# SBUF layout of a two-block transformer kernel: small tensors first, tiles at chosen offsets modulo 1024 bytes

## The reference

```python
x = first_block(x, ...)     # 1 layer: x += rms_norm(concat(attention(h), mlstm(h) gated) @ w_out)
                            #          x += rms_norm(square(relu(rms_norm(x) @ w_up)) @ w_down), d_ff 4096
x = second_block(x, c, ...) # 2 layers: mod = silu(c) @ ada_w + ada_b; differential attention (4 heads),
                            #   31-tap depthwise convolution, both gated and projected; then
f_gate, f_up = jnp.split(h2 @ w_ffn_in[l], 2, axis=-1)          # d_ff 2816
x = x + (1.0 + gate2) * ((jax.nn.silu(f_gate) * f_up) @ w_ffn_out[l])
```

## Time and profile before

| | |
|---|---|
| median of 3 runs | 1080.71 us (1077.39, 1080.71, 1085.57) |
| profiled execution, its time and span | 1080.6 us |
| granted TensorE clock, mean | 0.994 |
| PE busy / PE weight loads busy | 1058.0 us / 1007.3 us |
| DVE / ACT / POOL busy | 833.6 us / 525.7 us / 29.8 us |
| HBM read | 227.29 MB, 211 GB/s over the span |

### The profile page before, as it was taken

One profiled execution on the slowest core, in us unless ns is written; L12 is line 12 of the kernel. 1 busy time (PEld: TensorE's weight loads), 2 busy tenths in 40 slices (PEclk: granted clock), 3 DMA queues, 4 the chain that ended last, 5 costly groups with the idle time before them and its releaser, 6 DMA issues.

```text
span 1080.6 us, 19232 instructions
## 1 busy us (share of the span) xinstructions
PE 1058.0 (98%) x8174; PEld 1007.3 (93%) x8174; DVE 833.6 (77%) x1117; ACT 525.7 (49%) x625; POOL 29.8 (3%) x54
## 2 busy tenths in 40 slices
PE   7999999999999999999999999999999999999998
PEld 6878899999998989989999999999898899999998
DVE  5878699988775899968898887869999576555552
ACT  5554665554424544554644433464456455444441
POOL 5100000000000010000000000000000000000000
PEclk9999999999999999999999999999999999999998
DMA  8566348889893464428599998846442375666551
GB/s 278 166 215 235 117 176 298 281 288 307 292 353 116 161 200 130 145 88 303 182 368 311 331 335 295 271 135 230 161 156 79 118 254 184 197 190 193 173 175 39
DMA packets 137473, 230.37 MB, mean 213 GB/s; under 512 B 7107, under 2 KB 60715, under 8 KB 137389
## 3 DMA queue, kind: packets, MB, share of 16 engines
q1 hardware_dynamic: 135060, 227.05, 62.1%
q0 software_dynamic: 1408, 0.79, 0.4%
q10 hardware_dynamic: 921, 1.32, 0.4%
HBM read 227.29 MB, written 1.06 MB: 211 GB/s over the span
## 4 chain that ended last, share of the span: by engine, by line
PE 71%; DVE 18%; ACT 7%; DMA 2%; issue 1%; SPq 1%; DVEq 0%; POOL 0%; ACTq 0%
PE mm L435 66%; DVE lo L1296 7%; DVE cacc L1386 5%; ACT hi L840 3%; PE mm L478 1%; DMA raw<-in_w_in_dram 1%; DMA raw<-in_w_out_dram 1%; ACT pB L919 1%; DVE sB L1394 1%; DVE qk L1413 1%; DVE hf L1411 1%; DVE qk L1412 1%; DMA swap<-qk 1%; PE pv L576 1%; PE pa L542 0%
## 5 line engine op out<-in xcount | busy, mean ns | idle before, releaser
L435 PE MATMUL mm<-act_hi,hi 128*128 128x256 f32 x1760 | 489.1, 282 | 5.8 <-ACT act_hi L908 2.3
L435 PE MATMUL mm<-act_hi,lo 128*128 128x256 f32 x1760 | 484.2, 279 | 0.0
L435 PE MATMUL mm<-act_lo,hi 128*128 128x256 f32 x1760 | 467.5, 279 | 0.0
L1296 DVE TENSOR_TENSOR lo<-raw,hi 128x2048 fp32r<-128x2048 f32 (+1 forms) x159 | 359.6, 2265 | 133.0 <-ACT hi L840 130.3
L840 ACT ACTIVATE hi<-raw 128x2048 fp32r<-128x2048 f32 (+1 forms) x159 | 300.2, 1891 | 247.3 <-PE mm L435 194.4
L435 PEld LDWEIGHTS mm<-act_hi,hi 128*128 128x128 f32 x1760 | 331.4, 188 | 11.5 <-issue 7.1
L435 PEld LDWEIGHTS mm<-act_hi,lo 128*128 128x128 f32 x1760 | 331.9, 189 | 0.3
L435 PEld LDWEIGHTS mm<-act_lo,hi 128*128 128x128 f32 x1760 | 321.0, 188 | 0.0
L435 PE MATMUL mm<-u_hi,hi 128*128 128x256 f32 x608 | 171.9, 283 | 0.0
L435 PE MATMUL mm<-u_hi,lo 128*128 128x256 f32 x608 | 171.4, 282 | 0.0
L435 PE MATMUL mm<-u_lo,hi 128*128 128x256 f32 x608 | 171.4, 282 | 0.0
(11 more groups left out here) (280 smaller groups left out, 908.6 us busy)
## 6 DMA issues: line engine op xcount, KB each, us to landing
ada_raw<-in_ada_w_dram SPq DMA_DIRECT2D x128, 384.0 KB, 5.4
raw<-in_w_ffn_in_dram SPq DMA_DIRECT2D x88, 512.0 KB, 5.2
raw<-in_w_in_dram SPq DMA_DIRECT2D x39, 1024.0 KB, 5.3
raw<-in_w_ffn_out_dram SPq DMA_DIRECT2D x20, 1024.0 KB, 5.9
raw<-in_w_up_dram SPq DMA_DIRECT2D x16, 1024.0 KB, 6.4
raw<-in_w_down_dram SPq DMA_DIRECT2D x16, 1024.0 KB, 7.5
raw<-in_w_out_dram SPq DMA_DIRECT2D x12, 1024.0 KB, 5.8
raw<-in_w_in_dram SPq DMA_DIRECT2D x16, 512.0 KB, 5.9
```

Source lines behind the costliest of these rows:

```text
L435: ins = pe.matmul(o, w[:, kk, fs], a[:, k, :], start=(k == 0 and i == 0 and f % 2 == 0), stop=(ends and i == len(pairs) - 1), skip_group_c ...
L1296: v(dve.tensor_tensor(lo[:, c % RING, 0:nk, :], raw[:, c % RING, 0:nk, :], hi[:, c % RING, 0:nk, :].bitcast(F32), ALU.subtract), "lo_done")
```

## The change

The tensors are allocated in another order, and three unused ones are put in. First come the constants and small tensors; then `line_pad` (608 bytes of a partition), after which `raw`, `hi`, `lo`, `ada_raw`, `ada_acc` and `x` begin at multiples of 1024 bytes; then `act_pad` (256 bytes), after which `act_hi` and `act_lo` begin 256 bytes past such a multiple; then, behind `tabs`, `mix_pad` (256 bytes), after which the stage tensors and `u_hi` and `u_lo` begin 512 bytes past one. `wg`, `gbias` and `acol` go to the end of the stage `mixA`. The highest byte in use rises by about 1.1 KB. Before, the weight rings began 128 bytes past a multiple of 1024, `act_hi` and `act_lo` 192, `u_hi` and `u_lo` 416, `att_hi` and `att_lo` 544. No instruction, wait, size or order of work is changed.

```diff
@@ -235,19 +235,7 @@
         pa = ps("pa", [P, GF])
         pv = [ps(f"pv{i}", [P, GF]) for i in range(3)]
 
-        raw = sb("raw", [P, RING, CK, GF])
-        hi = sb("hi", [P, RING, CK, GF], F32R)
-        lo = sb("lo", [P, RING, CK, GF], F32R)
-        ada_raw = sb("ada_raw", [P, ADA_RING, ADA_W])
-        ada_acc = sb("ada_acc", [P, LAYERS, ADA_W])
         cst = sb("cst", [P, C_ALL])
-        x = sb("x", [P, KD, S])
-        act_hi = sb("act_hi", [P, KD, S], F32R)
-        act_lo = sb("act_lo", [P, KD, S], F32R)
-        hf = sb("hf", [P, 4, S])
-        sq = sb("sq", [P, KD, S])
-        rstd = sb("rstd", [P, 2, S])
-        tabs = sb("tabs", [P, 2, 2 * S])
         parT = sb("parT", [P, NROW])
         adabT = sb("adabT", [P, NMOD + ADA_P])
         modT = sb("modT", [P, NMOD])
@@ -258,8 +246,23 @@
         nlam = sb("nlam", [P, LAYERS])
         gain0 = sb("gain0", [P, KD])
         token_root = sb("token_root", [P, TT])
-
-
+        sb("line_pad", [P, 152])
+        raw = sb("raw", [P, RING, CK, GF])
+        hi = sb("hi", [P, RING, CK, GF], F32R)
+        lo = sb("lo", [P, RING, CK, GF], F32R)
+        ada_raw = sb("ada_raw", [P, ADA_RING, ADA_W])
+        ada_acc = sb("ada_acc", [P, LAYERS, ADA_W])
+        x = sb("x", [P, KD, S])
+        sb("act_pad", [P, 64])
+        act_hi = sb("act_hi", [P, KD, S], F32R)
+        act_lo = sb("act_lo", [P, KD, S], F32R)
+        hf = sb("hf", [P, 4, S])
+        sq = sb("sq", [P, KD, S])
+        rstd = sb("rstd", [P, 2, S])
+        tabs = sb("tabs", [P, 2, 2 * S])
+
+
+        sb("mix_pad", [P, 64])
         mixA = ExitStack()
         qk1 = sb("qk1", [P, KD, S], on=mixA)
         v1 = sb("v1", [P, TT, GF], on=mixA)
@@ -272,15 +275,12 @@
         mqk = sb("mqk", [P, 4, S], on=mixA)
         mv = sb("mv", [P, TT, GF], on=mixA)
         mo = sb("mo", [P, 4, S], on=mixA)
-        wg = sb("wg", [P, KD, F0 + MH], on=mixA)
         att = ExitStack()
         att_hi = sb("att_hi", [P, 4, S], F32R, on=att)
         att_lo = sb("att_lo", [P, 4, S], F32R, on=att)
         att.close()
         hng = sb("hng", [P, KD, S], on=mixA)
-        gbias = sb("gbias", [MH, 2], on=mixA)
         gate = sb("gate", [4, 8, S], on=mixA)
-        acol = sb("acol", [P, TT, 4], on=mixA)
         start = ExitStack()
         rows = sb("rows", [P, P], on=start)
         adab = sb("adab", [P, P], on=start)
@@ -300,6 +300,9 @@
         pM = sb("pM", [P, 2, 3 * P], on=mixA)
         emA = sb("emA", [P, 2, S], on=mixA)
         lams = sb("lams", [1, 16], on=mixA)
+        acol = sb("acol", [P, TT, 4], on=mixA)
+        gbias = sb("gbias", [MH, 2], on=mixA)
+        wg = sb("wg", [P, KD, F0 + MH], on=mixA)
         hmA = qk1[:, 0:2, :]
         mixA.close()
         mixB = ExitStack()
```

## The result

The changed kernel takes 1096.13 us (median of four runs, 1095.98 to 1096.73), the kernel before 1079.05 us (1072.90 to 1085.57) beside it. The ratio is 1.0177, with a 95% interval of 1.0126 to 1.0228: slower, though the interval doesn't say whether by more than 2%. The spread is a result too: 12.7 us before, 0.8 us after.

A forecast was written before the change was run, and what follows sets the result against it. Outside attention, the number of line 435 matmuls times their spacing was taken to bound the kernel. Gains of 10.5 us (u) and 6.3 us (act), all else nothing, summed to 16.8 us less: 1064 us, range 1040 to 1093.

The forecast's parts named there:

- What bounds the kernel: Outside attention, the number of line 435 matmuls times their start-to-start spacing, 113.3 to 120.0 ns for 256 columns.
- Two levels for the same addresses, chosen at an interruption: Act's matmuls step at 113.3 or 117.7 ns with the same addresses; the level seems chosen anew after an interruption.
- two streams of reads that lock: Line 435 matmuls: moving-tile and weight-tile reads lock in one of two phases, 4.4 ns apart for act; a reading, unproved.
- term 1: u's matmuls, moved from an odd 32 to a round start, all reach 113.3 ns: 10.5 us gained.
- term 2: Act's matmuls at the high level, 117.7 ns, fall to 113.3, less one long stretch: 6.3 us gained.
- Rival D: Line 435 matmuls: distance between the two tiles counts, not roundness; slower, 1091 us; chance 0.18.
- The slices' own period, 512: Slices of 128 weights are 512 bytes, so distances from weight to moving tile repeat modulo 512.
- The bound under term 2: Worst case for act's matmuls on the path: all go to 120.0 ns, 17.5 us lost.
- u's 1.7 us in term 1: Worst case for u's matmuls: all go to 120.0 ns, a loss of 1.7 us.
- Term 3: Everything else, VectorE, ScalarE, token-major and full fp32 matmuls, taken at nothing; 192 token-major matmuls under 2 us.
- Rival C: The change does nothing; line 435's levels come from the phase after each interruption alone: 1081 us; chance 0.12.

The follow-up runs named there:

- m2_phases: Matmul streams only, both blocks left out, six phases per distance: 113.3 ns in five of six at distance 192, two of six at 64; 120.0 in all six at 0.
- k1_shift128: The changed kernel with all large tensors another 128 bytes further, distances kept: 1097.99 us, ratio 1.0155.
- m1_distances: Streams of 60 fp32r matmuls only, both blocks left out, weight and moving tiles at varied offsets: 120.0 ns a step at distance 0, 116.7 and 117.8 at 288.
- k2_old_distances: The changed kernel's order, weights at a multiple of 1024, act back at 64 and u at 288 past one: 1081.50 us, ratio 1.0026.
- b4_after_knock: The changed kernel with one extra warming matmul behind the two sums after the first group of up: 1096.98 us, ratio 1.0141.
- k3_both_64: The changed order with act and u both 64 past a multiple of 1024, no `mix_pad`: 1083.86 us, ratio 1.0030.

## Why the prediction was wrong

I forecast 1064 us and a range of 1040 to 1093; it is 1096.
- What bounds the kernel was right: the steps of the line 435 matmuls carried all of the change, waits and durations stood still, and outside them no stage moved by more than the 1.9 us of the first 150. Two levels for the same addresses, chosen at an interruption, held up as well (m2_phases). That they are two streams of reads that lock stays a reading.
- The step that failed is the choice in term 1, that u "moves from an odd 32 to a round start" and comes down to 113.3, and with it term 2, that act's high level falls: u and act both went to 120.0. Roundness of a start does nothing (k1_shift128, m1_distances). What counts is the distance modulo 256 bytes. I had two distances with two levels each and drew the line through the starts; the same rows fitted the distance, and I gave that 0.18. The sum came out 16.8 us faster where the medians are 17.1 slower: a wrong sign, not a wrong size.
- Rival D had the right quantity and the wrong sizes. It took the nearest known distance, 288, for act's 256, and for u's 512 half of the gain that att's 116 ns would give. There is no nearness here: in the streams distance 0 has 120.0 alone and 32 bytes further there is 116.7 to 117.8, and 192 and 224 are 113.3 (or 117.8) and 118.3. Both new distances are 0 modulo 256. The slices' own period, 512, which I wrote down, would have told me that at least u's weight tile and moving tile now start alike.
- The bound under term 2 was the real outcome: all act at 120.0 for 17.5 us, with u's 1.7 us in term 1, in sum 19.2 us or 1100. Medians give 17.1, the two spans 13.4. I had these ends in hand and cut the range short of them at 1093. Of the 5.8 us between the working and the spans, 1.9 were won in the first 150 us, in part by the clock, and about 2 of act's in the projections of layer 0 (384 matmuls, 2.6 us slower by themselves) were given back by 495 us; I had counted those as on the path. The other 1.9 I can't place.
- I set the profiled span equal to the median. The changed kernel's span is 1094.0 in a run of 1096.1, so some 2 us lie around a span. If the same holds before, the profiled execution took about 1082.7, which is 3.6 above the later median of 1079.05, and that is the gap between 13.4 and 17.1.
- Term 3 held: k2_old_distances shows the new order at nothing. The token-major matmuls went from 233 to about 228 ns a step, worked out from the start times of lines 478 and 481: 1 us of 192 matmuls, the size I had given. The 128x512 operations on VectorE and ScalarE stayed at 688 and 620 ns.
- Rival C, that the change does nothing because the levels come from the phase alone, fell with the result itself and with m1_distances; b4_after_knock only adds that the extra matmul finds no lower level at distance 0.
- My prediction set a rule on C's side: the Trainium skill ("SBUF — State Buffer", Who interferes with whom) lets PE wait on no one and gives its moving operand and its weight load read ports independent of each other. The runs don't agree, if that means one speed at every address: the distance between these two tiles alone is worth up to 6.7 ns on 113.3.
- The formula N / 2.4 + 2.5 ns of the Trainium skill ("TensorE: Matmul & The Clock Gate", Back-to-back issue gap), 109.2 for 256 columns, is given there for an isolated matmul, which my prediction left out. The bf16 streams meet it at 109.2, and no fp32r stream of 256 columns does.

## What to carry to other kernels

If a kernel lives on one instruction, divide a stretch by its count in every stage before costing a change: equal code at two steps means that something besides the code sets the step, and the worst step seen anywhere is a real outcome for the whole kernel. In fp32r streams of this shape put the distance between moving and weight tile at 192 modulo 256 bytes and keep it off 0; rounding all tensors up to multiples of 256 is just what puts it at 0. At 64 the low level exists but came seldom, and moving u there gained nothing (k3_both_64). Two pads, 160 bytes in all, took 1.2% off here. One idle matmul at an interruption may give a long stretch another phase, better or worse; here that is one traced execution and no sure gain.

## What the runs showed that I had not expected

- The step of an fp32r stream (256 moving, 128 weight columns) goes by the distance modulo 256 bytes: 120.0 at 0 and 96, 116.7 to 117.8 at 32 (in the kernel 120.0 as well), 113.3 or 117.8 at 64 and 192, 118.5 to 120.0 at 128, 117.4 at 160, 118.3 at 224. bf16 (109.2) doesn't depend on it at eight distances, nor full fp32 (215.8) at three.
- A level, once drawn, holds for more than a thousand matmuls (1,056 at 113.3 in one stage, 1,440 at 117.7 in two). It would account for the 12.7 us over which the kernel before spreads, and the loss of the choice for the 0.8 us of the changed one; with one trace of each this is argued and not shown.
- 512 moving columns of fp32r have their own order: 226.7 ns at distance 0, 232.2 to 234.4 at 32, 128, 96, 160, 192 and 224, 228.8 to 229.0 at 64. There, 0 is the best place. In this kernel these are the 192 token-major matmuls only, and the change took them from distance 192 to 0: 233 to 228 ns.
- Fewer than 256 moving columns don't pay in fp32r: 224, 192, 160 and 64 columns all step by 111.7 ns at full granted clock.
